# Seven projections of the mixer, each as seven products of half its size

## What is computed

```python
def mixer_block(u, cos, sin, w_in, conv_w, q_norm_g, k_norm_g, w_conv_out, w_attn_out, w_o):
    proj = u @ w_in
    cb, cc, cx, q, k, v, gc, ga = split_columns(proj)
    z = depthwise_conv_centred(cc * cx, conv_w)
    y_conv = (cb * z) @ w_conv_out
    q = rmsnorm(q.reshape(B, S, N_HEADS, HEAD_DIM_2), q_norm_g)
    k = rmsnorm(k.reshape(B, S, N_KV_HEADS_2, HEAD_DIM_2), k_norm_g)
    ...
    y_attn = bidirectional_gqa(q, k, v) @ w_attn_out
    merged = jax.nn.sigmoid(gc) * y_conv + jax.nn.sigmoid(ga) * y_attn
    return merged @ w_o
```

## Time and profile before

| | us |
|---|---|
| median of 3 runs | 1962.69 (1962.51 to 1964.34) |
| profiled execution | 1961.86 |
| its span in the trace | 1960.1 |
| TensorE busy | 1607.0 (82%) |
| VectorE busy | 599.0 (31%) |
| ScalarE busy | 293.9 (15%) |
| GpSimd busy | 12.6 (1%) |

### The profile page before, as it was taken

The page is one execution under the profiler, slowest core; times in us unless marked ns, Lnnn a source line. Parts: engine busy times, 40 slices in busy tenths (PEclk is TensorE's granted clock), DMA queues, the critical chain, the costliest instruction groups (busy, mean ns, idle before and its releaser), DMA issues.

```text
span 1960.1 us, 20845 instructions
## 1 busy us (share of the span) xinstructions
PE 1607.0 (82%) x9050; PEld 964.0 (49%) x9050; DVE 599.0 (31%) x1390; ACT 293.9 (15%) x793; POOL 12.6 (1%) x37
## 2 busy tenths in 40 slices
PE   9999999999999999856555656565756565899999
PEld 7775567755688885322212222212222212457886
DVE  2663456634242312411201111101111101145533
ACT  0343313432012001100000000000000000223220
POOL 0000000000000000000000000000000000000000
PEclk9999999999999999987788888878888878999999
DMA  9751276433433564899999999999999999944200
GB/s 378 269 148 45 101 275 215 129 110 113 172 129 129 194 245 159 349 432 433 430 433 430 429 430 432 430 430 431 430 430 431 431 432 428 356 150 172 94 36 22
DMA packets 87782, 554.39 MB, mean 283 GB/s; under 512 B 4513, under 2 KB 11425, under 8 KB 74113
## 3 DMA queue, kind: packets, MB, share of 16 engines
q1 hardware_dynamic: 86544, 548.81, 69.7%
q0 software_dynamic: 1136, 4.10, 0.6%
HBM read 551.85 MB, written 1.05 MB: 282 GB/s over the span
## 4 chain that ended last, share of the span: by engine, by line
PE 62%; DMA 35%; DVE 2%; ACT 1%; issue 0%; SPq 0%; POOL 0%; ACTq 0%; DVEq 0%; POOLq 0%
PE bank L664 29%; DMA ring<-in_w 22%; DMA arena<-in_w 12%; PE bank L1118 8%; PE bank L691 6%; PE bank L673 6%; PE bank L1146 3%; PE bank L652 3%; PE bank L1436 1%; PE bank L862 1%; PE bank L796 1%; PE bank L776 1%; DMA prm<-in_pk 1%; DVE arena L2078 0%; PE bank L1389 0%; PE bank L1089 0%
## 5 line engine op out<-in xcount | busy, mean ns | idle before, releaser
L1118 PE MATMUL bank<-ring,arena 128*32 128x512 f32 x1216 | 289.4, 737 | 151.5 <-DMA arena<-in_w 91.4
L664 PE MATMUL bank<-arena,ring 128*128 128x256 f32 x1856 | 412.2, 380 | 1.0 <-DVE arena L2334 0.5
L664 PEld LDWEIGHTS bank<-arena,ring 128*128 128x128 f32 x1856 | 348.9, 190 | 50.9 <-issue 4.3
L1118 PE MATMUL bank<-arena 128*32 128x512 f32 x832 | 235.3, 737 | 108.4 <-DMA ring<-in_w 108.4
L1118 PEld LDWEIGHTS bank<-ring,arena 128*32 128x32 f32 x1216 | 72.4, 132 | 274.2 <-issue 274.2
L664 PE MATMUL bank<-ring,arena 128*128 128x512 f32 (+3 forms) x520 | 205.2, 544 | 1.8 <-DVE arena L2446 1.0
L1118 PEld LDWEIGHTS bank<-arena 128*32 128x32 f32 x832 | 57.0, 132 | 195.8 <-issue 195.6
L664 PEld LDWEIGHTS bank<-ring,arena 128*128 128x128 f32 x520 | 96.2, 190 | 84.5 <-issue 72.3
L691 PE MATMUL bank<-ring,arena 128*128 128x512 f32 (+1 forms) x320 | 129.2, 561 | 1.9 <-DVE arena L1961 0.8
L1146 PE MATMUL bank<-ring,arena 128*32 128x512 f32 x576 | 114.1, 631 | 19.4 <-DMA arena<-in_w 11.8
L673 PE MATMUL bank<-arena,ring 128*64 128x256 f32 x1024 | 112.7, 380 | 0.0
(11 more groups left out here) (392 smaller groups left out, 1398.9 us busy)
## 6 DMA issues: line engine op xcount, KB each, us to landing
ring<-in_w SPq DMA_DIRECT2D x53, 4096.0 KB, 31.6
arena<-in_w SPq DMA_DIRECT2D x35, 4096.0 KB, 37.3
ring<-in_w_in SPq DMA_DIRECT2D x40, 2048.0 KB, 7.9
ring<-in_w_mod SPq DMA_DIRECT2D x6, 2048.0 KB, 12.6
ring<-in_w_out SPq DMA_DIRECT2D x6, 2048.0 KB, 7.9
arena<-in_w SPq DMA_DIRECT2D x6, 2048.0 KB, 12.2
ring<-in_w SPq DMA_DIRECT2D x6, 2048.0 KB, 8.0
ring<-in_w_out SPq DMA_DIRECT2D x16, 512.0 KB, 9.3
```

Source lines behind the costliest of these rows:

```text
L664: i = te.matmul(ps, lhsT, rhs, start=n0 + k == 0, stop=n0 + k == n - 1)
L1118: m = te.matmul(ps[32 * j:32 * j + 32, :], LM.xg[:, f, 128 * k + 32 * j:128 * k + 32 * j + 32], vs[j][:, 512 * (k % 2):512 * (k % 2) + 512 ...
```

## The change

Each of the seven projections is cut into 2x2 blocks: input features in halves (chunks 0 to 3, 4 to 7), output features in halves (the slots g = 0, 1), tokens in halves (`lo`, `hi`). In place of the eight products of such blocks it makes seven, P1 to P7, of differences and sums of blocks. One product fills one bank: 4 output blocks of 128 by 4 input chunks, 16 multiplications of 128x128 weights with 128 tokens. The names' order is unchanged, and ya joins the list: 49 branch steps, and 39 of attention, which begins its transposes at its 14th step (before: the 9th). P3, P4, P5, P7 use weight differences T2, T1, T3, T4 (2048 columns each). T1 to T3 of the next name are made by VectorE behind P4, P6 and P7 of the present one, T4 by GpSimd once T2 is there and the former P7 is done. The products' sums are VectorE's, except one copy (P1 to s1) on ScalarE. The four token sums are made once for the five products with u, again for zT and for oT. Branches use banks 0 to 3, attention 4 to 7. Squares and the scaling of q and k move from VectorE to ScalarE; the gates' tanh is one instruction over 2048 columns. T1, T2 and T4, s1 to s3 and y1 lie in ring slots 4 and 5, so the seven projections use slots 0 to 3, and units 2 and 3 go to slots 4 and 5 after ya.

```diff
-    for _ in range(48):
+    for _ in range(7 * len(SEVEN)):
...
-MIX_ATT = 34
+MIX_ATT = 39
+SEVEN = ("cc", "gc", "ga", "cx", "cb", "yc", "ya")
...
+            sums = [ar(21008 + 512 * k, 4, 128) for k in range(4)]
+            late_sums = [ar(o, 4, 128) for o in (18448, 23312, 23824, 24336)]
+            t1, t2 = (ring[:, 4, 2048 * k:2048 * k + 2048].rearrange("p (c n) -> p c n", n=512) for k in range(2))
+            t4 = ring[:, 5, 0:2048].rearrange("p (c n) -> p c n", n=512)
+            s1, s2, s3, y1 = (ring[:, 5, 2048 + 512 * k:2560 + 512 * k].rearrange("p (c n) -> p c n", n=128)
+                              for k in range(4))
...
+                for w in at.all(*([("used", users[i])] if users[i] else []),
+                                *([("used", users[i], "sums")] if users[i] and users[i][0] in SEVEN and users[i][1] == 0
+                                  else [])):
                     s.wait_ge(*w)
...
+                    load((name, g), (whole, w[:, :, o:o + 512]), slot=(2, 0)[k % 2] + g)
+            users[4], users[5] = ("T", 0), ("T", 1)
+            slot_of[("T", 0)], slot_of[("T", 1)] = 4, 5
...
+            s.wait_ge(*at.of("mm", "P", "cb", 7))
             s.wait_ge(*at.of("z", 7))
             unit(4, LM.early[2])
-            ring_unit(2, ("yc", 0))
-            ring_unit(3, ("yc", 1))
-            s.wait_ge(*at.of("ev", "yc", 7))
+            for w in at.all(("att2", "PE"), ("att2", "DVE"), ("att2", "ACT")):
+                s.wait_ge(*w)
+            for u in range(2):
+                unit(u, LM.early[u])
+            for g in range(2):
+                load(("wo2", g), (whole, wv[:, :, 512 * g:512 * g + 512]), slot=g)
+            s.wait_ge(*at.of("sum", "yc", 21))
             unit(5, LM.late)
+            s.wait_ge(*at.of("sum", "ya", 21))
+            for u, name in ((2, ("T", 0)), (3, ("T", 1)), (6, ("ya", 0)), (7, ("ya", 1)), (8, ("wo2", 0)), (9, ("wo2", 1))):
                 ring_unit(u, name)
...
+            def times(group, w, xT, b):
+                ps = fresh(*group, b=b)
+                for i in range(4):
+                    m = product(ps[:, 128 * i:128 * i + 128], [(w[:, c, 128 * i:128 * i + 128], xT[:, c, :]) for c in range(4)])
+                m.then_inc(*t.done("mm", *group))
+            def seven_products(name, n, xT, sums):
...
+                t.wait_ge(*at.of("w", (name, 0)))
+                if name == "yc":
+                    ready(("sum", "cb", 11))
+                times(("P", name, 1), w0[:, 0:4, :], xT[:, 0:4, lo], 7 * n % 4)
+                yield
+                if name == "yc":
+                    ready(("sum", "cb", 12))
+                times(("P", name, 2), w0[:, 4:8, :], xT[:, 4:8, lo], (7 * n + 1) % 4)
+                t.also("used", (name, 0))
+                yield
+                ready(("T", name, 2), ("S", {"yc": 1, "ya": 2}.get(name, 0)))
+                times(("P", name, 3), L2.t2, sums[1], (7 * n + 2) % 4)
+                yield
+                times(("P", name, 4), L2.t1, sums[0], (7 * n + 3) % 4)
+                yield
+                ready(("T", name, 3))
+                times(("P", name, 5), w1[:, 0:4, :], sums[2], (7 * n + 4) % 4)
+                yield
+                times(("P", name, 6), w1[:, 4:8, :], sums[3], (7 * n + 5) % 4)
+                t.also("used", (name, 1))
+                yield
+                ready(("T", name, 4))
+                times(("P", name, 7), L2.t4, xT[:, 4:8, hi], (7 * n + 6) % 4)
+                yield
             def mixer_branches():
                 every = both("uT", 0) + both("uT", 1)
                 ready(*every)
...
+                for n, name in enumerate(SEVEN):
+                    if name == "ya":
+                        ready(*[("ev", "pv2", qb, hd) for qb in range(2) for hd in range(0, 8, 2)])
+                    xT, sums = dict(yc=(L2.zT, L2.late_sums), ya=(L2.oT, L2.late_sums)).get(name, (L2.uT, L2.sums))
+                    yield from seven_products(name, n, xT, sums)
...
-                for _ in range(8):
+                for _ in range(13):
...
+                banks.base = banks.width = 4
...
-                ready(*[("mg", ch) for ch in range(8)])
+                ready(("sum", "ya", 11), ("sum", "ya", 12))
...
+                ready(("sum", "ya", 21), ("sum", "ya", 22))
...
+                    ready(("mm", "P", name, 1), *([("sum", old, 11)] if old else []))
+                    se.copy(L2.s1, heads(bank("P", name, 1)[:, :], 128)).then_inc(*a.done("ev", "P", name, 1))
+                    yield
+                    if old in ("gc", "ga"):
+                        dst = L2.gcT if old == "gc" else L2.gaT
+                        ready(*[("sum", old, part) for part in (11, 12, 21, 22)])
+                        se.activation(dst, dst, ACT.Tanh, scale=0.5).then_inc(*a.done("gate", old))
+                    for _ in range(6):
+                        yield
...
+                    se.activation(L2.qr[:, tt, :], L2.qk[:, tt, :], ACT.Square).then_inc(*a.done("sq", "qk2", tt))
...
+                a.wait_ge(*at.of("rs", "qk2"))
+                for tt in range(2):
+                    q3 = L2.qk[:, tt, :].rearrange("p (a b) -> p a b", b=128)
+                    for hd in range(10):
+                        m = se.activation(q3[:, hd, :], q3[:, hd, :], ACT.Identity, scale=L2.r10[:, tt, hd:hd + 1])
+                    m.then_inc(*a.done("scaled", "qk2", tt))
...
+                if k == 1:
+                    ready(("mm", "P", old, 4) if old else ("used", ("os", 1, 1)))
+                    ve.tensor_tensor(L2.t1, w1[:, 0:4, :], w0[:, 0:4, :], ALU.subtract).then_inc(*v.done("T", name, 1))
+                if k == 2:
+                    ready(("T", name, 1), *([("mm", "P", old, 3), ("T", old, 4)] if old else [("used", ("os", 1, 1))]))
+                    ve.tensor_tensor(L2.t2, w1[:, 4:8, :], L2.t1, ALU.subtract).then_inc(*v.done("T", name, 2))
+                if k == 3:
+                    ready(("T", name, 1))
+                    ve.tensor_tensor(w1[:, 0:4, :], w1[:, 4:8, :], w1[:, 0:4, :], ALU.subtract).then_inc(*v.done("T", name, 3))
+            def token_sums(n, xT, sums):
...
+                ve.tensor_tensor(s1, xT[:, 0:4, hi], xT[:, 4:8, hi], ALU.add).then_inc(*v.step())
+                ve.tensor_tensor(s3, xT[:, 0:4, lo], xT[:, 0:4, hi], ALU.subtract).then_inc(*v.step())
+                behind()
+                ve.tensor_tensor(s2, s1, xT[:, 0:4, lo], ALU.subtract).then_inc(*v.step())
+                behind()
+                ve.tensor_tensor(s4, xT[:, 4:8, lo], s2, ALU.subtract).then_inc(*v.done("S", n))
...
+                def part_sum(name, part, k, other, to_be=None):
+                    arr, l, h_ = arrays[name]
+                    chs, cols = slice(0, 4) if part in (11, 21) else slice(4, 8), h_ if part in (21, 22) else l
+                    to = arr[:, chs, cols]
+                    ps = heads(bank("P", name, k)[:, :], 128)
+                    ready(("mm", "P", name, k))
+                    behind()
+                    if name in work:
+                        both = other if to_be is None else to_be
+                        ve.tensor_tensor(both, ps, other, ALU.add).then_inc(*v.done("ev", "P", name, k))
+                        behind()
+                        if name in ("cx", "cb"):
+                            ve.tensor_tensor(to, to, both, ALU.mult).then_inc(*v.done("sum", name, part))
+                        else:
+                            gate = dict(yc=L2.gcT, ya=L2.gaT)[name][:, chs, cols]
+                            ready(("gate", dict(yc="gc", ya="ga")[name]), ("qr", 1))
+                            ve.scalar_tensor_tensor(to if name == "yc" else both, gate, 1.0, both, ALU.add, ALU.mult
+                                                    ).then_inc(*(v.done("sum", name, part) if name == "yc" else v.step()))
+                        if name == "ya":
+                            behind()
+                            ve.tensor_tensor(to, to, both, ALU.add).then_inc(*v.done("sum", name, part))
+                    else:
+                        ve.tensor_tensor(to, ps, other, ALU.add).then_inc(*v.done("ev", "P", name, k))
+                        v.also("sum", name, part)
+                def to_sum(dst, name, k, other, *after):
+                    ready(("mm", "P", name, k), *after)
+                    behind()
+                    ve.tensor_tensor(dst, heads(bank("P", name, k)[:, :], 128), other, ALU.add
+                                     ).then_inc(*(v.step() if k == 4 else v.done("ev", "P", name, k)))
+                ready(("z0",))
...
+                for n, name in enumerate(SEVEN):
+                    new = SEVEN[n + 1] if n + 1 < len(SEVEN) else None
+                    if name == "cb":
+                        tap(2)
+                    yield
+                    if name == "cb":
+                        tap(2)
+                    yield
+                    to_sum(L2.s2, name, 3, L2.s1, ("ev", "P", name, 1))
```

(74 more changed lines are left out.)

136 lines of the change are left out of this document (51 added, 85 removed).

## The result

| | before | changed | changed, second session |
|---|---|---|---|
| median, us | 1961.84 | **1957.6** | 1953.89 |
| lowest to highest, runs | 1960.91 to 1964.34, 12 | 1955.15 to 1960.21, 12 | 1953.32 to 1955.11, 5 |
| ratio to before, interval | | 0.9978 [0.9969, 0.9986] | 0.996 [0.9946, 0.9974] |
| profiled execution, its span | 1961.86, 1960.1 | 1957.38, 1955.7 | 1955.11, 1953.4 |

The change makes the kernel 4.2 us faster, less than half of the forecast 9.1. In the second session (before beside it: 1961.69) it was 7.8 us. Both times lie in the range of 1946 to 1960, and 1957.6 lies just inside the 1951 to 1958 of the forecast's case.

A forecast was written before the change was run, and what follows sets the result against it. The prediction took TensorE alone to bound the projections and attention; the later experts' stage, bound by loads, moves as a whole. -18.3 (pace) - 1.5 (handoffs) + 10.7 (waits) = -9.1 us, forecast 1953.6 us, range 1946 to 1960.

The forecast's parts named there:

- the forecast's case: Whole kernel: GpSimd and VectorE take turns with a T4 of 3.4 to 4.6 us, 1951 to 1958 us, chance 0.50.
- TensorE's pace: Seven projections: seven products of 3.57 us replace 27.62 us each, 2.6 us saved per projection, 18.3 us in all.
- the two old handoffs: TensorE's gaps of 0.5 us before yc and 0.97 us before w_o's product go, 1.5 us saved.
- cb's P6: In cb, TensorE waits 1.4 us for the bank of P2, whose sum stands behind the taps.
- the second block's probabilities: Attention's second query block: probabilities done at 143.3 instead of 140.9, so TensorE waits 2.5 us.
- products with v, heads 2 and 3: Second query block: the copy of transposed probabilities ends at 157.9, TensorE stands there at 152.2, a 5.7 us wait.
- ya's P3: In ya, TensorE waits 1.2 us for the token sums of oT.
- Turns: GpSimd's T4 (4.1 us) and VectorE's two-input SBUF instructions exclude each other; TensorE's waits sum to 10.7 us.
- Rival 3: Gain eaten: VectorE 10% longer, T4 of 4.5, stalls 19 us, 1962 us; or clock falls, some 3 us; chance 0.13.
- Rival 1: GpSimd and VectorE run freely side by side; stalls of 4.2 us, 1947.1 us; chance 0.27.
- Rival 2: T4 takes 7.2 us and VectorE bounds the mixer; turns cost 26 us, slower at 1969 us; chance 0.07.
- Rival 4: Experts' first units arrive late, so the shorter mixer does not move the experts; time near 1963 us; chance 0.03.

The follow-up runs named there:

- run 1568: Not a follow-up run: in "was to run 1568 times" it counts the instructions of the seven products' form on TensorE; it has no measured time.
- T4 after P2: Against the changed kernel, GpSimd's T4 also waits for its own name's P2; 1948.2 us, ratio 0.9933 to before.
- the lighter VectorE: Against T4 after P2 with ya's products one bank on: each chunk's first tap and the second block's probability multiplication moved to ScalarE; 1946.4 us, ratio 0.9925.
- the filled wait: Against the changed kernel, four unused 512-column multiplications on TensorE put in front of its longest wait; 1953.43 us, ratio 0.9961.

## Why the prediction was right, and where not

| term | forecast | trace |
|---|---|---|
| TensorE's pace | -18.3 | -18.3 |
| the two old handoffs | -1.5 | -1.7 |
| cb's P6 | 1.4 | 1.19 |
| the second block's probabilities | 2.5 | 2.03 |
| products with v, heads 2 and 3 | 5.7 | 5.55 |
| ya's P3 | 1.2 | 1.21 |
| w_o's first product | 0 | 0.99 |
| the clock at 1.2 GHz behind the longest wait | 0 | 2.2 |
| stretch | -9.1 | -6.9 |
| ahead of and behind the stretch | 0 | +2.4 |

**TensorE's own time** held, to 0.1 us. The work at full clock is 195.0 us where it was 213.3, and the page of before was enough for it: eight L955 gave the pace of a form that was to run 1568 times. Seven eighths of the products took 8.6% off the full-clock work and not 12.5, because the pace at 128 tokens is 3% worse than half of that at 256, and because a tenth of the stretch is attention.

**Turns** was the right choice between the two ends, made without a row that showed it. The Trainium skill's rule ("SBUF — State Buffer", section "Who interferes with whom") agrees with what was seen of two-input instructions here: 0.69 against 4.48 us beside a GpSimd sum, 0.69 beside a fill that reads nothing, the waiting in both directions (5.52 for 4.52). The rule as the prediction told it does not cover the L2394 with one tensor input that was held with T4 after P2 (4.69 for 0.35). The Trainium skill's 4497 ns for 2048 columns ("GPSIMD Engine Reference", section 3.1) stand against 4.52 measured. My 4.1 from the row of 576 columns was 9% low, and the line's 3.4 was 25% low.

**The four waits** came at the places named, with 9.98 us where 10.7 were forecast and 12.2 with a T4 of 4.5. The one hold-up that was looked for first, T4 holding cx's part 21, is there with 3.8 us for 3.4. Two errors lie against each other, so that the sum of the waits came this close is in part luck: T4 is longer than taken, and VectorE has 134.3 us of work where the prediction's terms add up to some 139.5 (its 145 has the gaps between instructions as well, which busy time leaves out). ScalarE has 32.66 for 37.

**The step that failed** is one sentence: that w_o's half 0 finds its sums ready. The sums are ready; the product needs a bank as well, and bank 0 is that of ya's P7, whose own sum (L2413, 0.70 us) must be out first. I had walked through the banks for cb, where it gave 1.4 us, and not for the last hand-over. In its place the trace shows 0.99 us, and moving the banks took it away.

**What was named and not put in the sum** is the clock. Rival 3 had 3 us for it behind the longest wait; it is some 2.2, and 2.5 in the second session's execution. It is a consequence of a wait that stood in the forecast at full length, so it belonged in the forecast and not in a rival with 0.13. TensorE before the change had no wait over 1 us in this stretch, so no row showed what 5.5 would do; the rows of 850 to 1600 us, at 0.82 with many gaps, were the nearest, and they pointed there.

**Rival 1** (free, 1947.1) is out, by the long instructions. **Rival 2** needs a T4 of 6.2 us; the doubled T4 shows its mechanism with 1976. (Its named waits add up to 25.7, not 26, which makes 1968.6 of the 1969.) **Rival 4** is out: w_o to the first expert product kept its 43.2 us, with no wait for a load in it, though four units are asked for later.

**From the trace to the median.** On the profiled execution, 1957.38 where 1952.8 was forecast, the gain of the stretch is 2.2 us short; the rest of the 4.6 is the 1.9 us at the start and 0.5 behind the mixer. In the second session, whose profiled execution is without the 1.9, the median is 1953.89 beside a forecast of 1953.6; that this is closer than the terms deserve is luck with the parts that the change doesn't touch. From the first expert product to the end the eleven executions took 1168.7 to 1170.9 us, before and both of the changed kernel above 1170.1, the others below 1169.8. That stage runs by the loads, and no row explains the 2 us. It stays open, and comparisons of medians within 2 us in this study carry nothing by themselves.

## What to carry to other kernels

Before giving part of VectorE's work to GpSimd, look at what VectorE does at that moment: a two-input GpSimd instruction on SBUF held every VectorE instruction with two SBUF inputs that started behind it here, and a TENSOR_SCALAR from SBUF too, until its own end, so that 2.28 us of work taken off VectorE cost it 3.7 to 4.4 in six places of seven. If it must be there, start it where VectorE reads PSUM or waits, even if that takes an added wait; better, give one-input work to ScalarE instead. When TensorE's work is shortened until a queue beside it sets the pace, walk that queue and the banks up to the very last hand-over, and add to a wait of 3 us or more what the clock takes behind it (1.6 to 2.5 us here for one wait).

## What the runs showed of the hardware that was not expected

- A single wait of 5.5 us in a stretch in which TensorE is otherwise busy was enough for 6.8 us at 1.2 GHz, and one of 4.1 us (T4 on VectorE) for 3.4 us; the cost was 2.2 to 2.5 and 1.6 us. The wait of 3.0 us with the lighter VectorE cost 1.6. Below that it was not the same each time: a wait of 2.9 us (T4 twice, at 628 us) left the clock at 2.4 GHz, and the wait of 2.0 us before the transposes left it there in four executions and was followed by 3.4 us at 1.2 GHz in a fifth (the filled wait), at a cost of 1.6 us.
- Filling 2048 columns on GpSimd takes 1.81 us, subtracting them 4.52. By proportion the 1.15 us for 576 columns give 4.1, which is 9% under the one and over twice the other.
- The clock from 15 to 19 us, among the kernel's first products, is 0.60 or 1.00 in executions of one and the same kernel, and the first P1 comes 1.8 us later with 0.60.
